# Four edits at the stage borders of a fused two-block float32 kernel: when weight chunks are rounded, when a norm and the rotation tables are computed, and where the first output tiles of linear attention are multiplied

## The reference, cut to what matters

```python
# block 1, layer 0: gated linear attention (4 heads), then a conv-FFN, for latent and context tokens
o = gla(q, k, v, g_forward) + gla_flipped(q, k, v, g_backward)
y = (rms_norm(o, norm_g) * silu(r)) @ gla_w_out            # the "gate", then the output projection
x = x + g1 * y
x = x + g2 * conv_ffn(modulate(x, ...), ffn_w_in, conv_w, conv_b, ffn_w_out)
# layer 1: neighbourhood attention for the latent tokens
q = modulate(x_lat) @ w_q          # queries of the 512 latent tokens only
k, v = modulate([x_ctx, x_lat]) @ w_k, w_v
... softmax, @ na_w_out, conv_ffn on the latent tokens, final rms_norm
# block 2, two layers: MLA, stick-breaking attention and retention, branch gates, MLP
cos_m, sin_m = rope_tables(positions, 32)    # used by MLA
cos_r, sin_r = rope_tables(positions, 64)    # used by retention
```

## Time and profile before

| | |
|---|---|
| median of 3 runs | 3929.17 us (3923.21 to 3929.26) |
| profiled execution | 3926.22 us; its span 3924.4 us |
| TensorE matmul busy | 3769.1 us, 96% of the span |
| weight loads into TensorE | 3081.2 us, 79% |
| VectorE, ScalarE, GpSimd busy | 1708.0, 1480.9, 239.6 us |
| mean granted TensorE clock | 0.982 of full speed |
| DMA | 333.95 MB, mean 85 GB/s |

### The profile page before, as it was taken

How to read it: one execution, slowest core, us unless ns; L and a number is a source line. 1 busy time by engine, 2 the same in 40 slices (tenths; PEclk the granted TensorE clock), 3 DMA queues, 4 the chain that set the end, 5 groups by cost and what they waited for, 6 DMA issues and landing times.

```text
span 3924.4 us, 45303 instructions
## 1 busy us (share of the span) xinstructions
PE 3769.1 (96%) x18912; PEld 3081.2 (79%) x18912; DVE 1708.0 (44%) x2614; ACT 1480.9 (38%) x2355; POOL 239.6 (6%) x191
## 2 busy tenths in 40 slices
PE   7998889999998999999989999999999999999998
PEld 6898767888887977788766768878886676887887
DVE  5326735544544136544445443343334444334332
ACT  5245423332323236323345533232324544224232
POOL 0000000000000000000000001120110000112011
PEclk8999989999999999999999999999999999999999
DMA  5330022333321222223311123323221122332332
GB/s 197 104 113 2 17 70 70 108 120 124 111 86 55 89 68 71 85 92 102 100 51 53 60 73 97 105 83 100 95 98 55 44 70 70 100 105 86 97 96 81
DMA packets 108701, 333.95 MB, mean 85 GB/s; under 512 B 11472, under 2 KB 26704, under 8 KB 108368
## 3 DMA queue, kind: packets, MB, share of 16 engines
q1 hardware_dynamic: 108496, 331.06, 26.4%
HBM read 327.35 MB, written 2.10 MB: 84 GB/s over the span
## 4 chain that ended last, share of the span: by engine, by line
PE 91%; DVE 5%; ACT 3%; issue 1%; DMA 1%; POOL 0%; SPq 0%; DVEq 0%; ACTq 0%
PE ps L599 67%; PE ps L635 6%; PE ps L683 2%; PE ps L618 2%; PE ps L644 1%; PE ps L1165 1%; PE ps L992 1%; PE ps L827 1%; PE ps L1013 1%; PE ps L1001 1%; PE ps L854 1%; DMA raw<-weights_d 1%; PE ps L1086 1%; PE ps L1089 1%; PE ps L1108 1%
## 5 line engine op out<-in xcount | busy, mean ns | idle before, releaser
L2067 DVE TENSOR_TENSOR wlo<-raw,whi 128x1024 fp32r<-128x1024 f32 (+3 forms) x643 | 740.7, 1157 | 982.9 <-ACT whi L1326 982.3
L1326 ACT ACTIVATE whi<-raw 128x1024 fp32r<-128x1024 f32 (+3 forms) x643 | 620.9, 977 | 798.0 <-PE ps L599 633.3
L599 PE MATMUL ps<-bh,whi 128*128 128x512 f32 x1248 | 495.4, 397 | 0.1
L599 PE MATMUL ps<-bh,wlo 128*128 128x512 f32 x1248 | 487.3, 390 | 0.8 <-DVE wlo L2067 0.8
L599 PE MATMUL ps<-bl,whi 128*128 128x512 f32 x1248 | 487.0, 390 | 0.0
L599 PE MATMUL ps<-ah,whi 128*128 128x512 f32 (+2 forms) x1424 | 420.2, 354 | 6.9 <-ACT whi L1326 6.9
L599 PE MATMUL ps<-ah,wlo 128*128 128x512 f32 (+2 forms) x1424 | 418.6, 353 | 0.9 <-DVE wlo L2067 0.8
L599 PE MATMUL ps<-al,whi 128*128 128x512 f32 (+2 forms) x1424 | 416.3, 351 | 0.0
L599 PEld LDWEIGHTS ps<-ah,whi 128*128 128x128 f32 x1424 | 245.6, 189 | 44.6 <-ACT whi L1326 8.7
L599 PEld LDWEIGHTS ps<-bh,whi 128*128 128x128 f32 x1248 | 235.0, 188 | 57.4 <-issue 7.1
L599 PEld LDWEIGHTS ps<-bh,wlo 128*128 128x128 f32 x1248 | 234.8, 188 | 51.2 <-DVE wlo L2067 1.6
(11 more groups left out here) (348 smaller groups left out, 6131.7 us busy)
## 6 DMA issues: line engine op xcount, KB each, us to landing
raw<-weights_d SPq DMA_DIRECT2D x543, 512.0 KB, 3.4
raw<-weights_d SPq DMA_DIRECT2D x48, 256.0 KB, 2.6
raw<-weights_d SPq DMA_DIRECT2D x44, 192.0 KB, 2.4
x<-nab_d SPq DMA_DIRECT2D x24, 256.0 KB, 2.7
x<-x_t_d SPq DMA_DIRECT2D x4, 1024.0 KB, 6.0
dt<-rtab_d SPq DMA_DIRECT2D x16, 256.0 KB, 2.9
out_d<-x SPq DMA_DIRECT2D x4, 512.0 KB, 3.1
nvb<-nv SPq DMA_DIRECT2D x6, 256.0 KB, 4.5
```

Source lines behind the costliest of these rows:

```text
L599: m = e.matmul(p[:, 0:n], tiles(w, i)[:, k, :], xs[:, x0 + k, c0:c0 + n], start=pi == 0 and k == 0 and ti == 0, stop=i == job and k == kt ...
L1326: e.activation(flat(WHI, j), raw(j), ACT.Copy).then_inc(q.did("hi", j))
L2067: e.tensor_tensor(flat(WLO, j), raw(j), flat(WHI, j).bitcast(F32), ALU.subtract).then_inc(q.did("lo", j))
```

## The change

It has four parts.

1. **Output tiles inside the last gate.** TensorE's new `lin_part` runs part of a chunk's eight tiles. After `outputs(3)` it runs tiles 0 to 2 of output chunk 0, the sum of gate half 0, tiles 3 to 5, the sum of gate half 1, tiles 0 to 5 of chunk 1; then tiles 6 and 7 of each (those of head 3). The squares of (head 3, half 1) and head 3's `go` get their own buffers, the two `gqe` buffers swap heads, the banks of `gla_w_out` start at (2, 3) in place of (0, 1), SyncE's wait for the loads is for `outputs(2)`, ScalarE makes the two high halves between the gate's steps, VectorE makes two low halves early.
2. **FFN start**: the call for the third chunk, and with it the rounding of the fourth and fifth, stands before the first tile's gating, on both engines and in both FFNs.
3. **Context norm late**: on both engines it comes after the third query chunk (its halves, and on ScalarE the copies of three query tiles), with buffers that lie beside the queries.
4. **Tables spread** over all eight output tiles: nothing at ct = 0, then the positions and first angle, reductions, and so on.

```diff
@@ weight_plan
     turn = turns(6, 2)
+    next(turn)
     for ct in range(8):
         S("gla_w_out", (0,), 0, 8, plain(128 * ct), next(turn))
@@ pe_program
+        def lin_part(i, V, ready, segs, k0, k1):
+            ps = [PS[b] for b in plan[i][6]]
+            for k in range(k0, k1):
+                if k == 0:
+                    for si, b in enumerate(plan[i][6]):
+                        bank(b, ("ev", i, si))
+                q.wait_ge(("hi", i), *ready(k))
+                for ti, (w, xs) in enumerate(((WHI, V.hi), (WHI, V.lo), (WLO, V.hi))):
+                    if ti == 2:
+                        q.wait_ge(("lo", i))
+                    for p, (c0, n) in zip(ps, segs):
+                        m = e.matmul(...)
...
-        for s in range(2):
-            gate(3, s)
-        q.note("end_gla", "pe")
+        ahead = [chunk("gla_w_out") for _ in range(2)]
+        lin_part(ahead[0], Y, y_ready, SEGS, 0, 3)
+        gate(3, 0)
+        lin_part(ahead[0], Y, y_ready, SEGS, 3, 6)
+        gate(3, 1)
+        lin_part(ahead[1], Y, y_ready, SEGS, 0, 6)
+        q.note("end_gla", "pe")
+        def gla_out(ct):
+            if ct < 2:
+                lin_part(ahead[ct], Y, y_ready, SEGS, 6, 8)
+            else:
+                lin("gla_w_out", Y, y_ready, SEGS)
@@ act_program
-        for n, s in enumerate((0, 0, 1, 1, 0, 1)):
+        for n, s in enumerate((0, 1, 0, 1, 0, 1)):
             next(gates[s])
-            if n in (0, 1):
+            if n in (1, 3):
                 high_half()
...
                         ia, iv = [chunk("ffn_w_in", m) for m in range(2)]
+                        following = chunk("ffn_w_in")
                         gate_in(ia, n)
                         value_in(iv, n)
                     else:
-                        gate_in(chunk("ffn_w_in"), n)
+                        gate_in(following if n == 1 else chunk("ffn_w_in"), n)
...
+        n_norm(0, lambda k: by_column(AH, k))
+        pair = [chunk("na_w_qkv", n) for n in range(2)]
+        third = chunk("na_w_qkv")
+        for ct, i in enumerate(pair + [third]):
+            evac_q(i, ct)
+        n_norm(1, lambda k: AH[:, k, 0:TC])
...
             for n in range(2):
-                yield
+                for _ in range(4 - 2 * n):
+                    yield
                 other_table("sin")
                 q.wait_ge(("ang", n))
                 e.activation(TAB[:, 2 * n + 1, :], RR, ACT.Sin)...
                 e.activation(RR, RR, ACT.Abs)...
                 e.activation(TAB[:, 2 * n, :], RR, ACT.Sin, ...)...
                 yield
@@ dve_program
+        q.wait_ge(("gat", 3, 0, 0), ("gat", 3, 0, 1), ("gyl", 2, 1, 0), ("gyl", 2, 1, 1))
+        low_half()
         gates = [gate(3, s) for s in range(2)]
-        for s in (0, 1, 0, 1):
+        next(gates[0])
+        low_half()
+        for s in (1, 0, 1):
             next(gates[s])
...
+            yield
             q.wait_ge(("pos",))
             e.tensor_copy(POSF, POSI[:, :])...
             for n, iname in enumerate(("inv_mla", "inv_ret")):
                 e.tensor_scalar(ANG, POSF, col(iname), None, ALU.mult)...
+                yield
                 e.tensor_scalar(KKt, ANG, ...); e.tensor_scalar(KKt, KKt, MAGIC, ...)
+                yield
                 for s, (c, src) in enumerate(((-C1, ANG), (-C2_, RR), (-float(C3), RR))):
                     e.scalar_tensor_tensor(RR, KKt, c, src, ALU.mult, ALU.add)...
                 e.tensor_scalar(RR, RR, 3.1415925, -3.1415925, ALU.min, ALU.max)    # "ang" n
                 yield
-                yield
+                if n == 0:
+                    yield
@@ sp_program
-        q.wait_ge(("gom", 3, 1, 1))
+        q.wait_ge(("gom", 2, 1, 1))
         weights(first("na_w_qkv") + LOOK + 8)
```

More of the change, by code:

```diff
@@ L415, in build @@
     KTOK = at("gktok", [128, 6, 128], F32, 27 * KB)
-    Os = [at(f"go{i}", [128, T0], F32, 39 * KB + 3 * KB * i) for i in range(2)]
+    Os = [[at(f"go{n}{i}", [128, T0], F32, o + 3 * KB * i) for i in range(2)] for n, o in enumerate((39 * KB, oA + 12 * KB))]
     GM = at("gmask", [128, 7, 128], U8, 45 * KB)
@@ L452, in build @@
     NP = ring("np", 8, oX0 + 16 * KB)
+    NNORM = [(ring(f"nnrs{b}_", 1, oX0 + (16 + 8 * b) * KB), ring(f"nntr{b}_", 3, oX0 + (18 + 8 * b) * KB)) for b in range(2)]
     NK = at("nk", [128, 8, T0], F32, oX0 + 32 * KB)
@@ L601, in lin @@
                                          skip_group_check=True)
+                m.then_inc(q.did("mm", i))
+        def lin_part(i, V, ready, segs, k0, k1):
[9 more added lines that the diff above has]
+                    for p, (c0, n) in zip(ps, segs):
+                        m = e.matmul(p[:, 0:n], tiles(w, i)[:, k, :], xs[:, k, c0:c0 + n],
+                                     start=k == 0 and ti == 0, stop=k == 7 and ti == 2, skip_group_check=True)
+            if k1 == 8:
                 m.then_inc(q.did("mm", i))
@@ L1545, in gate @@
             for e_ in range(2):
-                q.wait_ge(("go", h, e_, s), *(fa if before[0] < 0 else [("ggn", *before, 1), ("gnm", *before)]))
-                e.activation(SQO[e_][:, :], Os[e_][:, c0:c0 + 384], ACT.Square).then_inc(q.did("gsq", h, s, e_))
+                free = fa if before[0] < 0 else [("glm", 3, 1, 1)] if (h, s) == (3, 1) else [("ggn", *before, 1), ("gnm", *before)]
+                q.wait_ge(("go", h, e_, s), *free)
+                e.activation(squares_of(h, s, e_)[:, :], out_of(h, e_)[:, c0:c0 + 384], ACT.Square).then_inc(q.did("gsq", h, s, e_))
             yield
-            rs = SQO[0][:, :]
+            rs = squares_of(h, s, 0)[:, :]
             ln_exp()
@@ L1693, in act_program @@
         pair = [chunk("na_w_qkv", n) for n in range(2)]
-        for ct, i in enumerate(pair):
+        third = chunk("na_w_qkv")
+        for ct, i in enumerate(pair + [third]):
             evac_q(i, ct)
-        for ct in range(2, 8):
+        n_norm(1, lambda k: AH[:, k, 0:TC])
+        q.note("end_nnorm", "act")
+        fn = fence("end_nnorm")
+        for ct in range(3, 8):
             evac_q(chunk("na_w_qkv"), ct)
@@ L2058, in dve_program, with low_half @@
         last = [-1]
+        def low_half():
+            j = last[0] = last[0] + 1
+            q.wait_ge(("hi", j), *([("mm", j - NS)] if j >= NS else []), *([("gom", 3, 1, 1)] if 0 < j - CORE < 3 else []))
+            e.tensor_tensor(flat(WLO, j), raw(j), flat(WHI, j).bitcast(F32), ALU.subtract).then_inc(q.did("lo", j))
         def chunk(name, held=0, until=N):
@@ L2064, in chunk @@
             while last[0] < min(i - held + LOOK, until - 1, N - 1):
-                j = last[0] = last[0] + 1
-                q.wait_ge(("hi", j), *([("mm", j - NS)] if j >= NS else []))
-                e.tensor_tensor(flat(WLO, j), raw(j), flat(WHI, j).bitcast(F32), ALU.subtract).then_inc(q.did("lo", j))
+                low_half()
             return i
```

59 lines of the change are left out of this document (33 added, 26 removed).

## The result

The changed kernel takes 3905.6 us (median of 6 runs, 3903.9 to 3911.7) against 3927.9 for the kernel before beside it (6 runs, 3923.2 to 3929.3): ratio 0.9947, 95% interval 0.9934 to 0.996. A second set on another chip gave 3904.69 (5 runs, 3904.0 to 3906.9), ratio 0.9937 (0.9924 to 0.9951). The forecast was 3907, range 3898 to 3915. The profiled execution took 3905.22 us with a span of 3903.4, 21.0 less than before.

A forecast was written before the change was run, and what follows sets the result against it. The prediction took TensorE as the bound (91% of what ended last), with time won only where it idles or runs at a lower clock. Its terms -15.4 - 1.0 - 8.5 + 5.4 = -19.5 took 3926.2 to 3907 us, range 3898 to 3915.

The forecast's parts named there:

- the gate's margins fail: Last gate: TensorE still waits for a low half or head 3's halves; -10.7 in place of -15.4, 3911.4 us; chance 0.13.
- The two waits: FFN starts: TensorE's waits of 0.48 and 0.53 us for low halves go, worth 1.0 together.
- a tax: FFN starts: ScalarE's late start makes TensorE wait in 43 later tiles; at 1 us each 3949.7 us; chance 0.03.
- the old wait: Before the third query chunk: the 5.66 us idle goes, and 2.80 us of lower clock behind it.
- Part 4's gain: Second FFN's output: the wait behind the positions' load (3.89) and the lower clock after it (1.4) go, 5.3 us.
- Part 4's tail: End of block 1: last sine group delays tile 6's square by 6.5 us, and the clock falls; 10.7 us lost.
- the term for the squares: End of block 1: three of eight squares' sums run at the lower clock, 0.85 us more each, 2.5 together.
- The tail costs more: End of block 1: all eight squares' sums run at the lower clock, 15.0 us lost, 3911.0 us; chance 0.12.
- costs nothing: End of block 1: calls miscounted, last table group lies before the last tile; 10.7 us less, 3896.0 us; chance 0.08.

The follow-up runs named there:

- e9: The changed kernel with the old order of making high and low halves at both FFN starts: 3908.83 us, ratio 0.9944 to the kernel before.
- e8: The changed kernel with the context norm back ahead of the third query chunk: 3915.27 us, ratio 0.9962 to the kernel before.
- e2: The changed kernel with the table pieces placed as in the kernel before: 3902.47 us, ratio 0.9929 to the kernel before.
- e4: The changed kernel with 14 unused matmul calls in TensorE's pause at block 1's end: 3902.43 us, ratio 0.9930 to the kernel before.
- e5: The changed kernel with the last sine group two output tiles earlier: 3899.48 us, ratio 0.9920 to the kernel before.
- e11: The changed kernel with unused fill matmuls ahead of every stage's first pair of chunks, tables unchanged: 3886.04 us, ratio 0.9889 to the kernel before.

## Why the prediction was right, step by step

The total was right by 1.4 us (3907 and 3905.6), and the largest term by mechanism and size. That the total is so close is in part luck: the other terms came out better than forecast, and losses that no step had covered that up.

- **Part 1, forecast -15.4.** 19.28 against 19.24 forecast; no wait inside, no sum of 2.9 (1.29 each); margins as worked out. -15.1 where it reaches the first FFN. The rival "the gate's margins fail" is refuted.
- **Part 2, forecast -1.0 with 1.0 as the upper bound.** The two waits went as said, and by e9 they were worth 0.7 and 0.9. The term took the 0.48 and 0.53 in the brackets for the whole cost; the starts show more, so the bound was too tight. The rival "a tax" is refuted: no later tile waits.
- **Part 3, forecast -8.5, lower bound 5.7.** -9.09 and, undone, 7.6 to 7.8. The context norm started 19.8 us after the pair (1257.70, 1237.93; forecast 1271.7 less 1251.82, 19.9), took 7.3 in place of 7.8, and the sixth chunk never waited. What is above 8.5 is the clock behind the old wait, 3.4 in place of 2.8 (2.3 in e8).
- **Part 4's gain, forecast -5.3.** -5.93 (e2 against changed).
- **Part 4's tail, forecast +10.7.** +7.89. Against e2 it is +9.28. The mechanism is as forecast: the sine group ahead of the square, the pause near 8 (7.54), the first sums near 2 (2.07). Three sizes: the pause grew by 6.0 and not 6.5; the two first sums, 1.12 and 1.02 in e2, took 2.07 and 1.84, 1.8 more where the forecast had 1.7; the term for the squares, 2.5, is 0.2 (9.09 less 8.92). The baseline was misread there: e2 and e4 show 7.53 for these sums at the upper clock, so the 8.92 of the earlier trace rows were partly at the lower one already (0.84 over 9 us), and it can't be charged twice. "The tail costs more" and "costs nothing" are both refuted.
- **What no step had.** Block 2, which the change doesn't touch, took 3.45 more; the stretch of values and attention 1.27 less; the first pair of the second FFN 1.33 less (13.85, 12.52); and the first FFN took 1.18 more, though part 2 took a wait out of it. All but the first recur between kernels with the same code at the place. The short block 2 (1940.7) was seen in the one trace of the kernel before alone; the ten other kernels without fill ahead of the pairs have 1944.2 to 1945.5. Whether it was that execution's luck or belongs to the kernel is open.

Set against the forecast, 6.9 us more were won: 2.8 in the tail of part 4 and 0.6 in its gain, 0.6 in part 3, 0.3 in part 2's second wait, 1.3 in the pair and 1.3 in values and attention. And 5.4 less: 3.4 in block 2, 1.7 in the first FFN, 0.3 in part 1. The difference of 1.5 is that of -19.5 and -21.0.

## What to carry to other kernels

Work that no nearby product needs can be hung on the last tiles of a stage only where the stage's own closing chain (square, addition, sum, norm) is not queued behind it on the same engine: count the calls from the end and leave two tiles free. Take a wait's cost from the distance of starts, not from the idle time alone: 0.53 in the brackets was 0.9. Before a difference in a stage is put down to an edit, see whether it lies behind the edit's place in time, and whether a kernel that has the edit shows it too. Where a border's pause can't be shortened, idle matmuls on a free bank ahead of the next products kept the clock and were worth 17 to 19 us here, more than the largest edit; where the norm still feeds those products tile by tile, they brought nothing.

## What the runs showed of the hardware that was not expected

The same instructions take one of a few discrete times, by how TensorE's clock falls over them. Block 2 has twice the same stage of many small products (latent and stick-breaking attention). Its stretches before, first and second layer, and then after:

```profile
2046.00:2230.70 184.70, 177.91 (x988) 123.16 (x986) 89.12 (x262) 107.95 (x244) 3.88 (x3) 0.99 0.15 49
3011.20:3200.40 189.20, 182.57 (x990) 126.06 (x988) 89.29 (x262) 107.96 (x244) 3.89 (x3) 0.96 0.16 48
```

```profile
2021.50:2210.70 189.20, 182.58 (x989) 125.96 (x988) 89.28 (x262) 107.98 (x244) 3.88 (x3) 0.96 0.15 48
2991.00:3178.80 187.80, 181.00 (x989) 124.72 (x987) 89.28 (x262) 107.85 (x244) 3.88 (x3) 0.97 0.15 48
```

From one 96-matmul chunk to the next it took 206.63 and 211.03 before, 210.99 and 209.70 after, and 208.2 to 211.3 in the other eleven kernels: the kernel before had the shortest first layer of all. The stretch of values and neighbourhood attention took 220.5 in eight of the thirteen kernels' traces and 221.8 in five (before, e4, e5, e9, e11), with nothing between. The first pair of the second FFN took 13.8 in before, e8 and e9 and 12.3 to 12.6 in the eight others without fill ahead of it; the squares' sums at block 1's end took 7.53 in e2, 8.92 before and 9.09 in e5, behind the same pause of 1.55. What sets it was not found: the changed kernel itself had 210.99 and 209.70 in one run and 211.02 and 210.97 in another. One to two us a stage go with no edit, and 4 at most if the 206.63 was luck, which one trace can't show. This is the reason why edits worth 3 us are read at their own place here.
